# Row sums, the order around U and V, and gathered rows at more places

## What is computed

```python
h = _rmsnorm(x, norm1_g)                       # norm 1
zc, zq, zk, zv, zr, za, zga, zgb = _split_cols(h @ w_in)
a_out = silu(layernorm(depthwise_conv(zc))) @ w_conv_out
b_out = (rmsnorm(gla(q, k, v, lg)) * silu(zr)) @ w_gla_o
x = x + (sigmoid(zga) * a_out + sigmoid(zgb) * b_out) @ w_mix_out
# PEER on norm 2 of x, for every token t with its 128 experts e and gates g
act = gelu(einsum('tkd,td->tk', u_tab[e], hf))
x = x + einsum('tk,tkd->td', g * act, v_tab[e])
y = _rmsnorm(x, final_g)                       # norm 3
```

## Time and profile before

| what | us |
|---|---|
| median of 3 runs (lowest, highest) | 4889.77 (4887.19, 4899.76) |
| time of the profiled execution | 4888.54 |
| its span, first to last instruction | 4886.8 |
| TensorE busy | 4675.6 (96%) |
| VectorE busy | 2655.6 (54%) |
| ScalarE busy | 535.2 (11%) |
| GpSimd busy | 892.9 (18%) |

### The profile page before, as it was taken

One profiled execution on the slowest core, in us unless ns is written; L12 is line 12 of the kernel. 1 busy time (PEld: TensorE's weight loads), 2 busy tenths in 40 slices (PEclk: granted clock), 3 DMA queues, 4 the chain that ended last, 5 costly groups with the idle time before them and its releaser, 6 DMA issues.

```text
span 4886.8 us, 47196 instructions
## 1 busy us (share of the span) xinstructions
PE 4675.6 (96%) x18798; PEld 3394.6 (69%) x18798; DVE 2655.6 (54%) x4623; ACT 535.2 (11%) x1220; POOL 892.9 (18%) x691
## 2 busy tenths in 40 slices
PE   8999999999999999899999999999999989999995
PEld 7888888888756566566667678888888734444442
DVE  3433300018658576635555467775777755545555
ACT  1111200001111101110000111111222200000000
POOL 1000000000111212003333231112333222222222
PEclk9999999999999999999999999999999999999997
DMA  4334334553776758548889788778899899999997
GB/s 162 145 137 144 143 144 167 193 188 123 242 269 221 296 204 315 200 168 354 346 340 358 273 334 317 269 279 293 329 335 333 312 393 414 413 373 417 417 417 292
DMA packets 237853, 1352.17 MB, mean 277 GB/s; under 512 B 43185, under 2 KB 43441, under 8 KB 131138
## 3 DMA queue, kind: packets, MB, share of 16 engines
q1 hardware_dynamic: 143778, 665.97, 37.0%
q0 software_dynamic: 93856, 683.19, 36.0%
HBM read 1308.38 MB, written 40.16 MB: 276 GB/s over the span
## 4 chain that ended last, share of the span: by engine, by line
PE 56%; DMA 23%; DVE 14%; issue 4%; ACT 1%; POOL 1%; POOLq 0%; SPq 0%; DVEq 0%; ACTq 0%
PE ps L357 30%; PE ps L632 11%; DMA RING<-in_peer_v,table 7%; DMA RING<-in_peer_u,table 7%; PE ps L553 5%; DVE CUR L836 4%; DMA RING<-in_peer_v,X 4%; DVE RING L830 4%; DMA RING<-in_peer_u,X 4%; PE ps L495 3%; DVE BIG L1102 2%; PE ps L559 1%; PE ps L373 1%; DMA out<-BIG 1%; PE pm L402 1%
## 5 line engine op out<-in xcount | busy, mean ns | idle before, releaser
L357 PE MATMUL ps<-X,BIG 128*128 128x320 f32 (+1 forms) x5632 | 1400.1, 410 | 7.1 <-DVE BIG L1200 6.5
L357 PEld LDWEIGHTS ps<-X,BIG 128*128 128x128 f32 x5632 | 1070.8, 191 | 320.1 <-issue 18.1
L836 DVE SCALAR_TENSOR_TENSOR CUR<-RING,wexp,CUR 128x2048 f32<-128x2048 f32 x320 | 752.1, 2350 | 397.5 <-DMA RING<-in_peer_v,table 292.4
L830 DVE CUSTOM_DVE_ANT_0 RING<-RING,CUR 128x2048 f32<-128x2048 f32 x320 | 729.7, 2289 | 413.9 <-DMA RING<-in_peer_u,table 278.5
L632 PE MATMUL ps<-X,RA 128*128 128x256 f32 x4096 | 902.9, 381 | 5.4 <-DMA RA<-in_uT 4.0
L632 PEld LDWEIGHTS ps<-X,RA 128*128 128x128 f32 x4096 | 777.3, 191 | 112.2 <-DMA RA<-in_uT 4.3
L1800 POOL DMA_INDIRECT RING<-in_peer_u,table x256 | 364.9, 1426 | 1335.4 <-DVE hidden L830 991.5
L1800 POOL DMA_INDIRECT RING<-in_peer_v,table x256 | 363.0, 1418 | 1132.9 <-DVE CUR L836 814.4
L655 PE MATMUL ps<-RA,BIG 128*128 128x512 f32 x1024 | 489.7, 601 | 23.0 <-DMA RA<-in_peer_v 14.8
L655 PE MATMUL pm<-RA,BIG 128*128 128x512 f32 x1024 | 481.6, 592 | 0.0
L655 PEld LDWEIGHTS ps<-RA,BIG 128*128 128x128 f32 x1024 | 191.5, 191 | 279.4 <-issue 200.7
(11 more groups left out here) (291 smaller groups left out, 2923.8 us busy)
## 6 DMA issues: line engine op xcount, KB each, us to landing
BIG<-in_w_in_b SPq DMA_DIRECT2D x64, 2048.0 KB, 8.9
RA<-in_uT SPq DMA_DIRECT2D x256, 512.0 KB, 5.5
RA<-in_peer_v SPq DMA_DIRECT2D x256, 512.0 KB, 9.4
BIG<-in_w_gb_b SPq DMA_DIRECT2D x16, 2048.0 KB, 8.4
BIG<-in_w_ga_b SPq DMA_DIRECT2D x16, 2048.0 KB, 8.2
BIG<-in_w_gla_o_b SPq DMA_DIRECT2D x16, 2048.0 KB, 10.1
BIG<-in_w_mix_b SPq DMA_DIRECT2D x16, 2048.0 KB, 9.8
BIG<-in_w_q_b SPq DMA_DIRECT2D x16, 2048.0 KB, 9.3
```

Of the source, the lines that this page charges most:

```text
L357: last = pe.matmul(bank[:, 0:n], w[:, k, j * P:(j + 1) * P], src[:, k, 0:n], start=(k == 0), stop=(k == kt - 1))
L830: row_used.on(dve.tensor_tensor_reduce(out=row, in0=row, in1=h2cur[0:n, :], scale=1.0, scalar=0.0, op0=ALU.mult, op1=ALU.add, accum_out=hi ...
L836: row_used.on(dve.scalar_tensor_tensor(out=cur[0:n, :], in0=row, scalar=wexp[0:n, par, k:k + 1], in1=cur[0:n, :], op0=ALU.mult, op1=ALU.ad ...
```

## The change

It touches these things:

- **Row sums.** For norm 1, the head norms, the mean and the variance, VectorE first adds up the feature tiles (`tensor_reduce`, `row_sums`), and TensorE makes one matmul with ones in place of 4, 8 or 16 (norm 1: four, one for each quarter).
- **Norm 2.** The squares are made in three parts, two of them during `mix`; the normed rows are written and transposed in quarters.
- **U.** `G_AT` is one lower. From then on VectorE does in each block: `gate_tokens`, argument, one-hots, last factor, and then rows. Before it was argument, `gate_tokens`, rows, last factor, one-hots. The paced amounts are 3.9 and 2.8 below `G_AT` - 1, and 4.5 from there.
- **V.** The first block's `pm` half starts before U's last block is finished on VectorE. The last two blocks are done first for token tile 0, then for tile 1. The residual and `final_g` are loaded in 12 pieces.
- **The end.** Each tile's sums, squares, norm and store follow by themselves, in pieces.
- **Rows at more places.** Three places of 2.4 in each sample chunk, two of 9.6 in `gates(1)`.
- **The change of token set.** The square goes to the ring, `final_g` is loaded earlier, and the next set's activation is loaded before the output is stored.

```diff
-G_AT = NB - PT // 4
+G_AT = NB - PT // 4 - 1
@@ TensorE
-            def column_sums(src, n, *key, kt=KT):
+            def column_sums(src, n, *key):
+                pe.wait_ge(*sums_ready.at(*key))
                 bank = banks.take(pe, *key)
-                for k in range(kt):
-                    last = pe.matmul(bank[:, 0:n], ones, src[:, k, 0:n], start=(k == 0), stop=(k == kt - 1))
-                ps_done.on(last, *key)
+                ps_done.on(pe.matmul(bank[:, 0:n], ones, src, start=True, stop=True), *key)
...
-                            pe.wait_ge(*conv_loaded.at(g))
-                            column_sums(conv[g], n, "mean", g, kt=CT)
+                            column_sums(mean_s[g], n, "mean", g)
...
+            def v_product(b, half, t):
+                m = 2 * NB + 2 * b + half
+                pe.wait_ge(uv_loaded[slot_of[m]].sem, loads_of[m])
+                for q in range(2):
+                    last = pe.matmul((ps, pm)[t][:, 2 * half + q, :], H[:, b, t * P:(t + 1) * P],
+                                     vhalf[slot_of[m]][:, q * 512:(q + 1) * 512], start=(b == 0), stop=(b == NB - 1))
+                return last
             pe.wait_ge(*gm_ready.at(PT // 4 - 1))
...
+            for half in range(2):
+                v_product(0, half, 1)
+            pe.wait_ge(*h_ready.at(NB - 1))
+            for half in range(2):
+                v_half.on(v_product(0, half, 0), 0, half)
+            for b in range(1, NB - 2):
...
+            for t in range(2):
+                for b in range(NB - 2, NB):
+                    for half in range(2):
+                        last = v_product(b, half, t)
+                ps_done.on(last, "tile", t)
@@ VectorE
+            def row_sums(dst, src, *key):
+                sums_ready.on(dve.tensor_reduce(dst, src.rearrange("p k n -> p n k"), AX.X, ALU.add), *key)
+            def x_row_sums(g):
+                for i in range(4):
+                    dve.wait_ge(*sq1_ready.at(g, i))
+                    row_sums(x_sums[g][:, i, :], sq1[g][:, 4 * i:4 * i + 4, :], "ms1", g, i)
+            def head_sums(g, h):
+                dve.wait_ge(*osq_ready.at(g, h))
+                row_sums(rms[g], sq[g], "ms", g, h)
...
                     if b:
                         sample_state(h, b - 1)
+                    if b in (2, 4, 6):
+                        run(work, 2.4)
...
+                if h:
+                    head_sums(g, h - 1)
                 if g:
                     spare((h, "kq"), 24.0)
...
             def gates(g):
+                head_sums(g, HEADS - 1)
+                if g:
+                    spare((0, "gates1"), 9.6)
...
+                dve.wait_ge(*conv_loaded.at(g))
+                row_sums(mean_s[g], conv[g], "mean", g)
                 center(g)
                 finish(g, HEADS - 1)
+                if g:
+                    spare((0, "gates2"), 9.6)
                 layer_norm(g)
...
             for b in range(NB):
...
+                if b > G_AT:
+                    gate_tokens(b - 1 - G_AT, b)
                 dve.wait_ge(*sq_u.at(b))
                 arg_u.on(...)
-                if b > G_AT:
-                    gate_tokens(b - 1 - G_AT, b)
                 spare((b, "u"), 0.0)
-                if b < G_AT:
-                    paced(work_1, 3.6)
-                paced(work, 2.0 if b < G_AT else 4.2)
+                if b < G_AT - 1:
+                    paced(work_1, 3.9)
+                    paced(work, 2.8)
+                elif b < NB - 2:
+                    onehots(b + 1 - G_AT)
...
                 h_ready.on(ins, b)
                 banks.free(h_ready, "u", b)
-                if G_AT - 1 <= b < NB - 1:
-                    onehots(b + 1 - G_AT)
-            gate_tokens(PT // 4 - 1, NB)
+                if b >= G_AT - 1:
+                    paced(work, 4.5)
@@ ScalarE
+            def resid_squares(g, part):
+                made, cols = ((3, slice(0, 1024)), (6, slice(1024, 1792)), (7, slice(1792, 2048)))[part]
...
+                    if i in (4, 7):
+                        resid_squares(g, i // 7)
                 norm2(g)
@@ GpSimd
+                if m % ROWS == 2 and t:
+                    pool.wait_ge(*ss_g.at(t - 1))
...
+                if m - 3 in last_u:
+                    gain_load(t)
@@ SyncE
-                if m == 2 * NB + 24:
-                    for t in range(2):
-                        x2_back.dma(sp.dma_start(x2b[:, t, :], x2_d[2 + t]), *((t,) if t == 0 else ()))
+                i = (m - 2 * NB - 48) // 8
+                cols = slice(512 * (i % 4), 512 * (i % 4) + 512)
+                if (m - 2 * NB) % 8 == 0 and 0 <= i < 8:
+                    x2_back.dma(sp.dma_start(x2b[:, i // 4, cols], x2_d[2 + i // 4, :, cols]), *((i,) if i < 7 else ()))
```

More of the change, by code:

```diff
@@ L176, in trunk @@
         rn = [part_of(CUR, 0, n) for n in N]
+        x_sums = [part_of(CUR, 1024, 4, n) for n in N]
         qT, kT, bT = ([rb(i * 640, 2, n) for n in N] for i in range(3))
@@ L368, in spent @@
                 weight_spent.append(ps_done.n)
-            def column_sums(src, n, *key, kt=KT):
+            def column_sums(src, n, *key):
+                pe.wait_ge(*sums_ready.at(*key))
                 bank = banks.take(pe, *key)
-                for k in range(kt):
-                    last = pe.matmul(bank[:, 0:n], ones, src[:, k, 0:n], start=(k == 0), stop=(k == kt - 1))
-                ps_done.on(last, *key)
+                ps_done.on(pe.matmul(bank[:, 0:n], ones, src, start=True, stop=True), *key)
             def norm1(g):
+                bank = banks.take(pe, "ms1", g)
                 for i in range(4):
-                    pe.wait_ge(*sq1_ready.at(g, i))
-                column_sums(sq1[g], N[g], "ms1", g)
+                    pe.wait_ge(*sums_ready.at("ms1", g, i))
+                    last = pe.matmul(bank[:, 0:N[g]], ones, x_sums[g][:, i, :], start=(i == 0), stop=(i == 3))
+                ps_done.on(last, "ms1", g)
             def za(g):
@@ L1235, in mix @@
                         dve.wait_ge(*resid_loaded.at(g))
+                    if i == 5 and g == 0:
+                        x_row_sums(1)
                     for s in range(LAST[g]):
@@ L1250, in norm2 @@
                     n = rows(c)
-                    dve.wait_ge(*ss2_done.at(g, c))
+                    dve.wait_ge(*ss2_done.at(g, c, 2))
+                    step(dve.tensor_reduce(small[0:n, c:c + 1], small[0:n, 12 + 3 * c:15 + 3 * c], AX.X, ALU.add))
                     ms2_ready.on(dve.tensor_scalar(small[0:n, 3 + c:4 + c], small[0:n, c:c + 1], 1.0 / D, EPS,
@@ L1349, in _ @@
                                  t, q)
-            for t in range(2):
-                dve.wait_ge(*ss3_done.at(t))
-                ms3_ready.on(dve.tensor_scalar(small[:, 14 + t:15 + t], small[:, 12 + t:13 + t], 1.0 / D, EPS, ALU.mult,
+                dve.wait_ge(*ss3_done.at(t, 3))
+                step(dve.tensor_reduce(small[:, 20 + t:21 + t], small[:, 12 + 4 * t:16 + 4 * t], AX.X, ALU.add))
+                ms3_ready.on(dve.tensor_scalar(small[:, 20 + t:21 + t], small[:, 20 + t:21 + t], 1.0 / D, EPS, ALU.mult,
                                                ALU.add), t)
-            dve.wait_ge(*fg_loaded.at())
-            for t in range(2):
                 dve.wait_ge(*root3.at(t))
-                step(dve.reciprocal(small[:, 16 + t:17 + t], small[:, 14 + t:15 + t]))
-                y_ready.on(dve.scalar_tensor_tensor(out=x2b[:, t, :], in0=x2b[:, t, :], scalar=small[:, 16 + t:17 + t],
-                                                    in1=final_g, op0=ALU.mult, op1=ALU.mult), t)
+                step(dve.reciprocal(small[:, 22 + t:23 + t], small[:, 20 + t:21 + t]))
+                for half in range(2):
+                    cols = slice(1024 * half, 1024 * half + 1024)
+                    y_ready.on(dve.scalar_tensor_tensor(out=x2b[:, t, cols], in0=x2b[:, t, cols],
+                                                        scalar=small[:, 22 + t:23 + t], in1=final_g[:, cols],
+                                                        op0=ALU.mult, op1=ALU.mult), t, half)
         @block.scalar
@@ L1680, in _ @@
                     squares(1)
-                else:
-                    for i in range(D // PAIR):
+                act.wait_ge(*ps_done.at("ao", g, D // PAIR - 1, 1))
+                for i in range(D // PAIR):
+                    if g:
                         serve((i, "mix"))
+                    if i in (4, 7):
+                        resid_squares(g, i // 7)
                 norm2(g)
@@ L1802, in gather @@
                     bass.IndirectOffsetOnAxis(ap=idx, axis=0), bounds_check=NEXP - 1, oob_is_err=True), m)
+            last_u = [TOPK * max(i for i, unit in enumerate(units) if unit[0] == t and unit[2] == "u") + TOPK - 1
+                      for t in range(3)]
             cur_load(0)
```

152 lines of the change are left out of this document (77 added, 75 removed).

## The result

The changed kernel takes 4841.69 us (median of 4 runs, 4834.42 to 4843.11); the kernel before took 4888.48 (4879.05 to 4899.76) beside it. The medians are 47 us apart, 0.96%. The ratio is 0.9885, with a 95% interval of 0.9865 to 0.9905, which is 46 to 66 us. So the change is about 1% faster. Ratios are of fast runs alone: one of the four executions of the run with rows at the old places, further down, took 22589 us and is left out of its ratio (the median of its other three is 4798.7). The forecast was 4762 with a range of 4725 to 4808. The sign was right, the size was not: of 127 us forecast, 47 came, and the time lies 34 us above the range.

The account below looks back on a forecast made before the run. V was taken as bound by VectorE's rows, with TensorE the bound after the change. Gains of 21 (column sums), 30 (U), 4 (change to V), 22 (V) and 50 (end) sum to 127 us, giving 4762 us, range 4725 to 4808.

Parts of the forecast that it names:

- Start, heads and gates of group 0, norms: Fewer column-sum matmuls gain 5.4 us at the start, 3.9 in heads, 7 in gates, 7.5 and 6.5 at norms.
- Group 1, where VectorE paces: Heads of group 1: reductions lengthen VectorE's list, added rows lie in its waits; 8 us lost (3 gained to 25 lost).
- Gates of group 1: Rows ahead of the mean's and variance's sums may delay them up to 6 and 7 us; 1 us lost (5 gained to 10 lost).
- U: Second part: one-hot waits go, blocks shrink from 8.67 to 8.2 us, 30 us gained (0 to 52); first part costs nothing.
- The change to V: Going from U to V, TensorE's 7.5 us wait for the last gates shrinks; 4 us gained (0 to 7).
- V: With 180 rows left, TensorE bounds V, and 256 KB pieces let the table through: 905 becomes 883, 22 us gained (12 to 26).
- The end: Behind TensorE's last pass only one tile is left: tail 10.7 us instead of 60.8, 50 us gained (45 to 51).
- three signs of being wrong: Wrong if rows still run at the end, U takes over 1000 us, or reductions of 1024 elements over 2.5 us.
- smaller ones: Expected: no row after about 700 us of V, no `peer_v` wait above 3 us, gates(1) sum waits of 6 to 13.
- The second one, gathers that pace U and group 1: Rival: late gathers, U and its end gain nothing, heads and gates(1) lose 20 us; 4807 us, chance 0.20.

Follow-up runs that it names:

- the run with rows at the old places: Changed kernel with rows only at the places and in the amounts of the kernel before, row sums and new order kept: 4799.1 us, ratio 0.9806.
- the run with VectorE's time alone: Changed kernel with each sample-chunk row of group 1 replaced by a VectorE reduction that loads nothing, the 12 rows done in V: 4795.2 us, ratio 0.9800.

## Why the prediction was right and wrong

- **Start, heads and gates of group 0, norms: right.** 25.1 us against 23.8, and 6.2 against 6.5 for norm 2 of group 1. The price of a strided reduction (1.9, 2.4 and 4.5 us for 1024, 1280 and 2560 elements) was 1.91, 2.37 and 4.44. The estimate by the Trainium skill's 1x figure (VectorE: DVE Perf Modes, The perf-mode tier table) was 1.2 us for 1024 and stays well below the trace. The Trainium skill's rule (same page, Rules for kernel authors) against tensor_reduce on a hot path did not decide here: without rows ahead of the sums TensorE waits for none of them in the gates.
- **Group 1, where VectorE paces: wrong, and this is the step that failed most.** The forecast had 8 us lost in the heads with an end of 25 us; 42 came. I named the traffic ("12 MB more pass while states are stored and loaded") and priced it with a guess between two ends instead of going through the chain: four times in each chunk store, wait, load on one queue, each transfer some 1.4 us longer in the last head. The 12 rows were called free, because they lie in VectorE's waits. They do lie there, and still cost 3.6 us each, on the DMA side. The other half of the step was right: heads without these rows take 859.4 us on average, 859.7 before, so neither the reductions nor the saved matmuls show.
- **Gates of group 1: right mechanism, wrong size.** Up to 6 us of wait for the mean and 7 for the variance were named, 9.7 and 6.1 came. The wait for a gather was allowed with 3 us and took 9.04. Without the rows the change would have gained here: 499.9 us on average against 508.1 before, 8 us; with rows 519.8. The eight rows thus cost 20 us, 2.5 each. The term was 1 us lost with an end of 10 (measured 9).
- **U: the wait removed, as said; the block mis-sized.** 31.8 us of waits went to 1.1. The mean block was to be 8.2 us, with 7.8 to 8.4 named, and was 8.41, 8.33 without the wait ahead of V. The step named late gathers and VectorE behind them; those came (55.7 us), but TensorE's own wait was for uT, which the argument did not have. With 1.5 rows a block it is 7.92, so the last rows packed into a block cost 34 us for 24, 1.4 each. The nine profiles with 4.5 lie between 969 and 988 us for U, so 8 us short is within their spread. The spread goes with the waits for uT: 16.6 us of them in the shortest U, 29.0 in the longest. U's first part took its added rows for nothing, as said (6.95 us a block, 6.94 before).
- **The change to V: half right.** The gates' last wait was 5.2 us in place of 7.5; the forecast allowed 1.5 to 7.
- **V: wrong.** Bound by TensorE, yes, and 180 rows at 4.2 us, yes. But "pieces of 256 KB should let the table through" failed: eight profiles with the loads early took 906 to 918 us in V (mean 913), in any form, six with them late 893 to 908 (mean 900). That is 14 of the 31 us, 22 in the best case. The kernel before had 906.1 with its loads early, so the step that failed is that pieces would gain anything where they stood. Even the best is above 883: its waits for peer_v are down to 4.3 us, and why the rest stays is open.
- **The end: right** (50.7 against 50), and so was its condition, that rows leave V, as the run with rows at the old places shows.
- **The signs named ahead.** None of the three signs of being wrong appeared: rows ended early, U took 985 us, a reduction 1.91. What missed were smaller ones: the last row came 753 us into V and not about 700, waits for `peer_v` went to 3.8 us and not 3, and waits for the gates' sums were 15.8 us and not 6 to 13. No sign named the states' loads, where most of the loss lay.
- **The rivals.** The second one, gathers that pace U and group 1, had the right kind of cause and 4807 us; it took 20 us for heads and gates together where 51 came. What no rival had is that SyncE's own loads are late beside the rows. In all, 34 + 8 us in group 1, 31 in V and 8 in U make the 81 us by which the forecast was too low. Rows at the old places alone come to 4799, and with the added rows in U but not in group 1, and the pieces late, to 4765: the plan of the prediction stands for U's rows and the end, not for group 1. That this is near 4762 is in part luck: V is 18 us above its forecast there, and the heads and gates, without their rows, 10 below.

What stays open: why the waits for uT differ between executions with the same U, 17 of V's 31 us, and whether the three places for the table matter in U's second part.

## What to carry to other kernels

A gap of the engine that does a piece of work is not free if the work's data has to pass while another engine's loads are on their way: ask of each place what is on the DMA queues there, above all a chain of store, wait and load. Here the same row cost 3.6 us of TensorE in the sample chunks, 2.5 ahead of the layer norm's sums, 1.4 as the second one in a block of U's second part. In U's first part 20 more cost nothing and 21 on top of them 0.3 us a block. In V 24 more cost nothing where the pieces ran beside rows anyway (914.3 us against 915.0), and 12 more cost 14 us where they ran on beside the late pieces. And a load without an early deadline, such as a residual for the end, belongs where the queues have become quiet; cutting it into pieces in the busy stretch changed the number of waits, not their sum.

## What the runs showed of the hardware

- Gathers of 1 MB beside a store and a load of 512 KB lengthened these from 5.3 and 4.3 us to 6.8 and 5.6 (median from issue to landing, last head's chunk), at a mean of about 240 GB/s in that stretch, far below the 414 GB/s that V moved. The mean rate of a stretch did not tell whether a chain of transfers was being held up.
- U's second part had late tables at 356 GB/s (24.1 us of waits), and at 329 GB/s, with 1.5 rows a block, few (5.1). U's first part had next to none at 366 GB/s (1.1).
- The strided reduction took 1.91, 2.37 and 4.44 us for 1024, 1280 and 2560 elements, 1.73 to 1.87 ns an element. A reduction along contiguous elements, 2240 in the run with VectorE's time alone, took 2.48 us, 1.11 ns an element. That the stride alone makes the difference is not shown: the strided one also writes a result for every 4 or 8 elements, the other one for every 320.
- In the last head's chunk the mean granted clock was 1.00 from 2039 to 2059 us, where TensorE had no wait over 0.7 us, and 0.68, between the two levels, from 2067 to 2083, which begins behind its wait of 4.34 us. Four passes took 3.67 us there and 1.93 before. Over the heads the clock was 0.95 with rows in the chunks and 0.97 in the run without: 23 us more of waits for states (30.4 against 7.4) came with 47 us more of time, of which 17 are busy time of TensorE. The Trainium skill (TensorE: Matmul & The Clock Gate, Why this matters for your kernels) has idle gaps bring the clock down; the trace agrees.

```profile
2059.61 1.93 PE L444 MATMUL pm<-BIG 128*64 128x512 f32 x4 [0.68 <-DMA BIG<-in_state_gla]
2067.80 3.33 PE L444 MATMUL pm<-BIG 128*64 128x512 f32 x4 [4.34 <-DMA BIG<-in_state_gla]
2076.40 3.67 PE L444 MATMUL pm<-BIG 128*64 128x512 f32 x4 [3.36 <-DMA BIG<-in_state_gla]
```
